# ScalarE issues the gate and up loads of the experts on its own queue, SyncE the down loads alone

## The chip, the cores and the metric

The kernel runs on 1 core of one Trainium2 chip. The metric is the device time of one execution in microseconds (us). Engines are named as the profile names them: PE (TensorE, the matmuls), PEld (its weight loads), DVE (VectorE), ACT (ScalarE), POOL (GpSimd) and SP (SyncE); a "q" behind a name is the engine's sequencer, which issues DMAs and waits on semaphores.

## What is computed

One step of a decoder layer over 264 tokens: 256 of a prompt and 8 samples. A token mixer with four branches comes first, then a mixture of 64 SwiGLU experts, of which every token takes 8, with one shared expert beside them. The part that matters here:

```python
def moe_ffn(h, router_w, router_bias, e_gate, e_up, e_down, s_gate, s_up, s_down):
    scores = jax.nn.sigmoid((h @ router_w).astype(jnp.float32))
    ...
    gates = jnp.zeros((n, N_EXPERTS), jnp.float32).at[jnp.arange(n)[:, None], idx].set(w)
    hg = jnp.einsum('nd,edf->nef', h, e_gate)
    hu = jnp.einsum('nd,edf->nef', h, e_up)
    act = jax.nn.silu(hg) * hu * gates[:, :, None].astype(h.dtype)
    routed = jnp.einsum('nef,efd->nd', act, e_down)
```

d is 1024 and f is 256, all in float32, so each expert has a gate, an up and a down matrix of 1,024 KB each, and the 64 experts together 201 MB. Every expert's weights are read from HBM once.

## The kernel before

The mixer and the routing take the first 350 us or so, and the change leaves them alone. After them the experts run as 64 jobs in 16 groups of four: job `4*i + j` is place `j` (0 to 3) of group `i`. The routing sorts the experts by how many tokens chose them, and the order of the jobs is written to `order_i`, one row of 64 integers; the first two jobs are experts 0 and 1. A job takes 128, 64 or 32 rows (CAP, HALF, QUARTER), a fixed size for each place. A middle group ("full group", i from 3 to 13) has rows of 128, 32, 64 and 32; the last group (i = 15) has four jobs of 32.

Weights go to `wexp`, which has four slots of 6,144 numbers per partition: gate in 0:2048, up in 2048:4096, down in 4096:6144. Job `4*i + j` uses slot `j`. Two semaphores a slot tell of landings: `gu_full[j]` (gate and up) and `down_full[j]`.

PE's order is written out by hand in `body` (line 1381 on): for each place `j` it computes `up(i, j)` (lines 1253, 1256, 1258 and 1259, by the size of the job) and in its middle turns the activation of the job before (`turn_act`, L898); then come the token list of the job four places on (L1206), the sums of a sheet at one place of each group (L1341), and the turning of gathered rows (`turn_rows`, L898 on `xn`); last is `down` of the job before (L1290, L1299, L1305 and L1308). So `down` of a job follows `up` of the next one. `up` counts `up_done` once, `down` counts `down_done` twice.

ACT goes beside it: `act_out` (L1660), `gate_out` (the silu, L1668), `rows_out` (L1652, half of the turned rows to `mid`) and `y_out` (L1682, L1685). DVE multiplies (L2248), copies the other half of the rows (L2229) and splits the outputs (L2263). POOL gathers the rows of tokens of a sheet from `h_table` to `xn` (L824), two sheets a group.

The loads come all from SP, on one queue. After the first four jobs' loads, `reload(i, s)` (line 679) runs for each job from 4 on: it loads the expert's number into a register, waits until `up` of the job four places before is done, and issues gate and up (L661, L662); then it waits until `down` of the job five before is done and issues the down load (L665) of the job before. The queue then holds gate, up, down of the job before, gate, up, and so on. After the last job come `turn_first_sums` (L1350, L1364), the last `down` and `last_sum` (L1316), final norm and the store.

Of the kernel before, what the change touches and what calls it, by code (L numbers as in the profile page):

```python
# [26 lines left out]
NE = 64  # L27
# [77 lines left out]
def bank_of(name):  # L105

    return (JOB[name] + FIRST_BANK) % NBANK, JOB[name] // NBANK
# [18 lines left out]
UNROLL = 4  # L126
# [31 lines left out]
def bass_decoder_step(nc, x_prompt, x_sample, state_conv, state_pool, state_conf, c_prompt, c_sample,  # L158
# [6 lines left out]
    with ExitStack() as ctx:  # L165
        def sb(name, shape, dt=F32):
            return ctx.enter_context(nc.sbuf_tensor(name, shape, dt))
# [3 lines left out]
        def sb_twin(name, shape):  # L171

            t = sb(name, shape)
            at = nc.sbuf_base - 4 * int(np.prod(shape[1:]))
            twins[name] = nc.alloc_sbuf_tensor_at(name + "_r", shape, F32R, offset=at)
            return t
# [5 lines left out]
        def sem(name):  # L182
            return ctx.enter_context(nc.semaphore(name))
# [5 lines left out]
        wexp = sb_twin("wexp", [P, UNROLL, SLOTF])  # L189
# [83 lines left out]
        order_i = sb("order_i", [1, NE], I32)  # L273
# [93 lines left out]
        S = {n: sem(n) for n in names}  # L367
        gathered = [sem(f"gathered{b}") for b in range(2)]
        gu_full = [sem(f"gu_full{s}") for s in range(UNROLL)]
# [6 lines left out]
        def await_full(eng, name):  # L376

            b, before = bank_of(name)
            eng.wait_ge(bank_full[b], before + 1)
            return psum[:, b, :]  # L380
# [5 lines left out]
        def await_freed(eng, name):  # L386

            b, before = bank_of(name)
            eng.wait_ge(bank_free[b], before + 1)
# [5 lines left out]
        def need(eng, sem_, value):  # L395

            if not isinstance(value, int) or value > 0:
                eng.wait_ge(sem_, value)
# [58 lines left out]
        def rows_used(i, j):  # L457

            if isinstance(i, int) and i == 0:
                return ROWS_OF_FIRST_JOB[j]  # L460
            if last_group(i):
                return QUARTER
            return (ROWS_OF_END_JOB if end_group(i) else ROWS_OF_LIGHT_JOB if light_group(i) else ROWS_OF_JOB)[j]
# [13 lines left out]
        def first_group(i):  # L477

            return isinstance(i, int) and i == 0

        def light_group(i):

            return isinstance(i, int) and 0 < i <= LIGHT_FIRST or end_group(i) or last_group(i)
# [26 lines left out]
        def sheet_of(i, s):  # L510

            return s if first_group(i) else 2 * i + 1 + s

        def buffer_of(i, s):

            return s % 2 if first_group(i) else 1 - s

        def next_sheet(i, j):

            if j == UNROLL - 1:  # L520
                return None if isinstance(i, int) and i == LAST else (i + 1, 0)
            if first_group(i):
                return (0, 2) if j == 1 else None
            return (i, 1) if j == (1 if light_group(i) else 0) else None

        def jobs_before_buffer(i, s):

            if first_group(i):
                return 1 if s == 2 else 0
            if s == 1:  # L530
                return UNROLL * i
            return UNROLL * (i - 1) + (2 if first_group(i - 1) or light_group(i - 1) else 1)
# [15 lines left out]
        def slots_of(i, j):  # L548

            return max(rows_used(i, j), HALF)  # L550

        gate_v = e_gate[0].rearrange("e (p k) f -> e p (k f)", k=KT)
        up_v = e_up[0].rearrange("e (p k) f -> e p (k f)", k=KT)
# [26 lines left out]
        def _(sp):  # L580
# [33 lines left out]
            for i, u in enumerate(SPLIT):  # L614
# [9 lines left out]
                n, at = divmod(i - FIRST_BRANCH, PER_BRANCH)  # L624
# [24 lines left out]
            def rows_of_expert(view, e):  # L649
                return view[e] if isinstance(e, int) else view[bass.ds(e, 1)].rearrange("e p n -> (e p) n")  # L650

            def expert_of(i, j):

                if isinstance(i, int) and i == 0 and j < FIXED:
                    return j
                at = UNROLL * i + j
                entry = order_i[0:1, at:at + 1] if isinstance(i, int) else order_i[0:1, bass.ds(at, 1)]
                return sp.value_load(entry, min_val=0, max_val=NE - 1)

            def load_gate_up(e, s):  # L660
                sp.dma_start(wexp[:, s, 0:2048], rows_of_expert(gate_v, e)).then_inc(gu_full[s], 16)  # L661
                sp.dma_start(wexp[:, s, 2048:4096], rows_of_expert(up_v, e)).then_inc(gu_full[s], 16)  # L662

            def load_down(e, s):
                sp.dma_start(wexp[:, s, 4096:6144], rows_of_expert(down_v, e)).then_inc(down_full[s], 16)  # L665
# [6 lines left out]
            for s in range(FIXED, UNROLL):  # L672
                e = expert_of(0, s)
# [2 lines left out]
                load_gate_up(e, s)  # L676
                load_down(e, s)

            def reload(i, s):
                n = UNROLL * i + s  # L680
                e = expert_of(i, s)
                sp.wait_ge(S["up_done"], n - 3)
                load_gate_up(e, s)
                pi, ps = (i if s else i - 1), (s - 1) % UNROLL
                if isinstance(pi, int) and pi == 0:
                    return
                before = expert_of(pi, ps)
                sp.wait_ge(S["down_done"], 2 * (n - 4))
                load_down(before, ps)

            for s in range(UNROLL):
                reload(1, s)
            with sp.Fori(2, NE // UNROLL) as i:
                for s in range(UNROLL):
                    reload(i, s)
            final = expert_of(NE // UNROLL - 1, UNROLL - 1)
            sp.wait_ge(S["down_done"], 2 * (NE - 4))
            load_down(final, UNROLL - 1)

            def extra(r, job, n):  # L700
                sp.wait_ge(S["x_xt"], n + 1)
# [13 lines left out]
            for m, t in enumerate(FINAL_ORDER):  # L715
                t0, n = TILES[t]
# [734 lines left out]
        def _(ac):  # L1451
# [171 lines left out]
            for m, t in enumerate(MIX_ORDER):  # L1623
                t0, n = TILES[t]
# [20 lines left out]
            def shared_silu(j):  # L1645
                b = await_full(ac, ("shared_gate", j))
                free(F(sh_silu[:, j, :], b[:, 0:TOK], ACT.Silu), ("shared_gate", j))

            def rows_out(i, s):
                ac.wait_ge(S["xt_done"], sheet_of(i, s) + 1)  # L1650
                need(ac, S["up_done"], jobs_before_buffer(i, s))
                F(xgT[buffer_of(i, s)][:, 0:4, :], psum[:, 5, :].rearrange("p (k c) -> p k c", k=4), ACT.Copy).then_inc(S["xgt_act"], 1)  # L1652

            def act_out(i, j):
                e = UNROLL * i + j
                n = rows_used(i, j)
                ac.wait_ge(S["tact_done"], e + 1)
                need(ac, S["down_done"], 2 * e - 2)
                at = HALF if n == QUARTER else 2 * P
                F(actT[:, j % 2, :, 0:n], psum[:, 2, 0:at].rearrange("p (h c) -> p h c", h=2)[:, :, 0:n], ACT.Copy).then_inc(S["actT_ready"], 1)  # L1660

            def gate_out(i, j):
                e = UNROLL * i + j
                n = slots_of(i, j)
                width = P if rows_used(i, j) == QUARTER else FE
                ac.wait_ge(S["up_done"], e + 1)
                need(ac, S["act_ready"], e - 1)
                F(silu[0:n, j % 2, 0:width], psum[CAP - n:CAP, j % 2, 0:width], ACT.Silu).then_inc(S["silu_ready"], 1)  # L1668
# [38 lines left out]
            def body(i, first=False, last=False):  # L1707
                for j in range(UNROLL):
                    prev = not (first and j == 0)
                    pi, pj = (i if j else i - 1), (j - 1) % UNROLL  # L1710
                    if prev:
                        act_out(pi, pj)
                    gate_out(i, j)
                    if next_sheet(i, j):
                        rows_out(*next_sheet(i, j))
                    if last and j:
                        raw_out(pj)
                    elif prev:
                        y_out(pi, pj)
# [2 lines left out]
            rows_out(0, 0)  # L1722
            shared_silu(1)
            await_full(ac, ("shared_up", 1))
            rows_out(0, 1)
            body(0, first=True)
            body(1)
            for i in range(2, LOOP_FROM):
                body(i)
# [17 lines left out]
            for m, t in enumerate(FINAL_ORDER):  # L1747
                n = TILES[t][1]
# [776 lines left out]
```

## Time and profile before

| | |
|---|---|
| median of 3 runs | 887.52 us (885.96 to 888.55) |
| the profiled execution | 888.6 us |
| its span, first to last instruction | 886.8 us |
| granted clock of TensorE, mean | 0.983 of full speed |
| PE busy | 838.4 us (95%) |
| DVE busy | 571.4 us (64%) |
| ACT busy | 309.3 us (35%) |
| DMA | 295.93 MB, mean 334 GB/s |
| the SP queue's part of it | 280.55 MB, 81.9% of 16 engines |

The time of the whole execution is compared with the median; the trace counts from the first instruction, so its times are read against the span. Busy PE means that matmuls are in its pipeline, not that it is at its peak. DMA-issuing instructions are not counted as busy time of an engine. "To landing" is the time from the issue of a DMA to the semaphore that tells that all of it has arrived. Line numbers are those of the kernel before; the change moves those behind it by a few.

### The profile page before, as it was taken

The page shows a single profiled execution, that of the slowest core. Times are in us where ns is not written, and L with a number is a line of the kernel's source. Part 1 is how long each engine was busy: PE and PEld are TensorE (multiplying, and loading weights), DVE is VectorE, ACT ScalarE, POOL GpSimd, SP SyncE. Part 2 cuts the span into 40 slices and gives each one's busy share as a digit, 9 for nine tenths or more (in the row PEclk, how much of TensorE's full clock was granted, in tenths as well). Part 3 has the DMA queues.
Part 4 walks back from the last instruction along what each step waited for, and adds up shares of the span by engine and source line. Part 5 has one row for each costly group of instructions (what it writes and reads, how often), then busy time and mean ns, then how long its engine had stood idle before and what let it go on. Part 6 is the DMA issues. An engine that isn't in the chain of part 4 may idle for free.

```text
span 886.8 us, 21212 instructions
## 1 busy us (share of the span) xinstructions
PE 838.4 (95%) x7938; PEld 638.9 (72%) x7938; DVE 571.4 (64%) x1431; ACT 309.3 (35%) x592; POOL 49.1 (6%) x92
## 2 busy tenths in 40 slices
PE   4799999999999999999999999999999999998794
PEld 2599999999999998757675656656665656566471
DVE  2458888899996787546664555546464655555555
ACT  3464444343428423022332323232232323222324
POOL 2010000000000000110000000000000000000000
PEclk9999999999999999899999999999999999999997
DMA  9995557788977645989999999999999999999961
GB/s 339 345 257 157 168 179 238 253 308 263 331 264 258 199 174 226 389 320 404 404 421 419 418 420 420 420 421 421 420 419 421 422 419 419 419 418 420 418 266 50
DMA packets 92711, 295.93 MB, mean 334 GB/s; under 512 B 7718, under 2 KB 45670, under 8 KB 67659
## 3 DMA queue, kind: packets, MB, share of 16 engines
q1 hardware_dynamic: 86139, 280.55, 81.9%
q0 software_dynamic: 6016, 13.10, 4.0%
q10 hardware_dynamic: 489, 1.33, 0.5%
q8 instruction: 48, 0.79, 0.4%
q14 instruction: 19, 0.16, 0.0%
HBM read 300.19 MB, written 4.14 MB: 343 GB/s over the span
## 4 chain that ended last, share of the span: by engine, by line
PE 69%; DVE 14%; DMA 12%; issue 2%; ACT 1%; SPq 1%; DVEq 0%; POOLq 0%; ACTq 0%
PE psum L894 19%; PE psum L1256 9%; DMA wexp<-in_e_up 9%; PE psum L1341 6%; PE psum L898 6%; PE psum L1253 6%; PE psum L1258 6%; PE psum L1299 4%; DVE mid L1922 4%; DVE wexp_r L1795 4%; PE psum L1290 3%; PE psum L1305 3%; DMA xn<-h_table,idx 2%; DMA wexp<-in_ada_w 2%; PE psum L1316 1%
## 5 line engine op out<-in xcount | busy, mean ns | idle before, releaser
L894 PE MATMUL psum<-xn_r,wexp_r 128*128 128x264 f32 x1024 | 193.8, 289 | 6.0 <-DVE hT_r L1833 6.0
L894 PEld LDWEIGHTS psum<-xn_r,wexp_r 128*128 128x128 f32 x1024 | 161.8, 191 | 8.4 <-issue 8.0
L894 PE MATMUL psum<-hT_r,wexp_r 128*128 128x264 f32 x512 | 146.4, 286 | 0.0
L1795 DVE TENSOR_TENSOR wexp_r<-wexp,wexp_r 128x1024 fp32r<-128x1024 f32 x88 | 106.6, 1217 | 22.1 <-ACT wexp_r L1505 21.7
L1505 ACT ACTIVATE wexp_r<-wexp 128x1024 fp32r<-128x1024 f32 x88 | 92.3, 1054 | 59.5 <-PE psum L894 44.3
L894 PEld LDWEIGHTS psum<-hT_r,wexp_r 128*128 128x128 f32 x512 | 98.0, 191 | 0.1
L1256 PE MATMUL psum<-wexp,mid 128*128 128x512 f32 x208 | 94.8, 600 | 0.6 <-DMA wexp<-in_e_up 0.6
L2187 DVE TENSOR_SCALAR idx<-psum 32x1 int32<-32x1 f32 (+2 forms) x62 | 13.4, 216 | 118.4 <-PE psum L1206 117.3
L1253 PE MATMUL psum<-wexp,mid 128*32 128x128 f32 x2112 | 76.3, 284 | 10.9 <-DMA wexp<-in_e_up 8.6
L2263 DVE TENSOR_TENSOR bc_r<-psum,xn_r 32x256 fp32r<-32x256 f32 (+2 forms) x136 | 65.9, 484 | 27.4 <-ACT xn_r L1685 17.5
L1253 PEld LDWEIGHTS psum<-wexp,mid 128*32 128x32 f32 x2112 | 58.8, 110 | 26.9 <-issue 15.1
L1256 PEld LDWEIGHTS psum<-wexp,mid 128*128 128x128 f32 x208 | 37.4, 190 | 48.5 <-issue 48.0
L894 PE MATMUL psum<-wexp_r 128*128 128x264 f32 (+1 forms) x512 | 71.5, 285 | 0.0
L1258 PE MATMUL psum<-wexp,mid 128*64 128x256 f32 x288 | 69.6, 385 | 0.3 <-DMA wexp<-in_e_up 0.3
L1259 PE MATMUL psum<-wexp,mid 128*64 128x256 f32 x288 | 69.6, 384 | 0.0
L894 PEld LDWEIGHTS psum<-wexp_r 128*128 128x128 f32 x512 | 66.8, 189 | 0.9 <-issue 0.9
L2305 DVE TENSOR_TENSOR mid<-mid,psum 128x264 f32<-128x264 f32 x120 | 50.7, 427 | 13.9 <-PE psum L1341 10.2
L1258 PEld LDWEIGHTS psum<-wexp,mid 128*64 128x64 f32 x288 | 36.9, 137 | 29.8 <-issue 12.9
L824 POOL DMA_INDIRECT xn<-h_table,idx x33 | 33.4, 1012 | 447.3 <-DVE idx L2187 209.2
L1341 PE MATMUL psum<-hT_r,mT_r 128*128 128x264 f32 x240 | 53.3, 304 | 0.6
L1668 ACT ACTIVATE hT<-psum 64x256 f32<-64x256 f32 (+2 forms) x64 | 20.8, 326 | 92.2 <-PE psum L1256 41.4
L1922 DVE SCALAR_TENSOR_TENSOR mid<-wexp,prm,mid 128x256 f32<-128x256 f32 x120 | 49.7, 474 | 0.0
(344 smaller groups left out, 1307.4 us busy)
## 6 DMA issues: line engine op xcount, KB each, us to landing
wexp<-in_e_gate SPq DMA_DIRECT2D x64, 1024.0 KB, 14.5
wexp<-in_e_up SPq DMA_DIRECT2D x64, 1024.0 KB, 17.5
wexp<-in_e_down SPq DMA_DIRECT2D x64, 1024.0 KB, 17.1
wexp<-in_w_in SPq DMA_DIRECT2D x32, 1024.0 KB, 6.3
mid<-in_ada_w SPq DMA_DIRECT2D x8, 2048.0 KB, 9.5
wexp<-in_w_branch SPq DMA_DIRECT2D x8, 1024.0 KB, 5.3
wexp<-in_ada_w SPq DMA_DIRECT2D x14, 512.0 KB, 10.7
wexp<-in_w_out SPq DMA_DIRECT2D x4, 1024.0 KB, 6.4
```

The costliest lines, as they stand in the source:

```text
L894: last = mm(out, a[x], b[y], start=start and x == y == 0, stop=stop and x == 1)
L898: return nc.tensor.transpose(out, src, ident[0:rows, 0:rows])
L1253: last = mm(psum[q * QUARTER:(q + 1) * QUARTER, j % 2, 0:P], x[:, k, :], w[:, k, 1 - q // 2, q % 2:FE:2], start=(k == 0), stop=(k == KT - ...
L1256: last = mm(psum[:, j % 2, :].rearrange("p (a f) -> p a f", a=2), x[:, k, :], w[:, k], start=(k == 0), stop=(k == KT - 1))
L1258: mm(psum[HALF:CAP, j % 2, 0:FE], x[:, k, :], w[:, k, 0], start=(k == 0), stop=(k == KT - 1), tile_position=(0, HALF))
L1259: last = mm(psum[0:HALF, j % 2, 0:FE], x[:, k, :], w[:, k, 1], start=(k == 0), stop=(k == KT - 1), tile_position=(0, 0))
L1341: last = mm(out, as_r(y[:, c * P:(c + 1) * P]), as_r(to_token[:, a, :]), start=((b, a) == sheets[0] and y is y_sheets[b][0] and not shared ...
L1505: F(as_r(high(u, q)), low(u, q), ACT.Copy).then_inc(S["w_hi"], 1)
L1795: V.tensor_tensor(as_r(low(u, q)), low(u, q), as_r(high(u, q)).bitcast(F32), ALU.subtract).then_inc(S["w_lo"], 1)
L1922: taps[c] = mark(V.scalar_tensor_tensor(dcv[:, c, 0:SEQ], gluP[:, c, h:h + SEQ], w, dcv[:, c, 0:SEQ], ALU.mult, ALU.add))
L2263: last = V.tensor_tensor(as_r(low[rows, a]), whole, as_r(high[rows, a]).bitcast(F32), ALU.subtract)
L2305: V.tensor_tensor(accT[:, c, :], accT[:, c, :], out, ALU.add).then_inc(S["sum_taken"], 1)
```

## The change

SP's `reload` is split. `reload_down` on SP waits until `down` of the job four places before is done (the last job that used the slot) and issues the down load of this job. A new `reload_gate_up` on ACT loads the expert's number and issues the two loads; it stands in ACT's `body` right behind `gate_out(i, j)` and is for job `j` of the next group. `gate_out` waits for `up` of the same slot's job, which was what SP waited for. ACT waits once for `order` to be written. The loads of jobs 0 to 3 stay on SP.

```diff
--- before.py
+++ after.py
@@ -676,26 +676,16 @@
                 load_gate_up(e, s)
                 load_down(e, s)
 
-            def reload(i, s):
-                n = UNROLL * i + s
+            def reload_down(i, s):
                 e = expert_of(i, s)
-                sp.wait_ge(S["up_done"], n - 3)
-                load_gate_up(e, s)
-                pi, ps = (i if s else i - 1), (s - 1) % UNROLL
-                if isinstance(pi, int) and pi == 0:
-                    return
-                before = expert_of(pi, ps)
-                sp.wait_ge(S["down_done"], 2 * (n - 4))
-                load_down(before, ps)
+                sp.wait_ge(S["down_done"], 2 * (UNROLL * (i - 1) + s + 1))
+                load_down(e, s)
 
             for s in range(UNROLL):
-                reload(1, s)
+                reload_down(1, s)
             with sp.Fori(2, NE // UNROLL) as i:
                 for s in range(UNROLL):
-                    reload(i, s)
-            final = expert_of(NE // UNROLL - 1, UNROLL - 1)
-            sp.wait_ge(S["down_done"], 2 * (NE - 4))
-            load_down(final, UNROLL - 1)
+                    reload_down(i, s)
 
             def extra(r, job, n):
                 sp.wait_ge(S["x_xt"], n + 1)
@@ -1659,6 +1649,14 @@
                 at = HALF if n == QUARTER else 2 * P
                 F(actT[:, j % 2, :, 0:n], psum[:, 2, 0:at].rearrange("p (h c) -> p h c", h=2)[:, :, 0:n], ACT.Copy).then_inc(S["actT_ready"], 1)
 
+            def reload_gate_up(i, j):
+
+                at = UNROLL * i + j
+                entry = order_i[0:1, at:at + 1] if isinstance(i, int) else order_i[0:1, bass.ds(at, 1)]
+                e = ac.value_load(entry, min_val=0, max_val=NE - 1)
+                for at, view in ((0, gate_v), (2048, up_v)):
+                    ac.dma_start(wexp[:, j, at:at + 2048], view[bass.ds(e, 1)].rearrange("e p n -> (e p) n")).then_inc(gu_full[j], 16)
+
             def gate_out(i, j):
                 e = UNROLL * i + j
                 n = slots_of(i, j)
@@ -1711,6 +1709,8 @@
                     if prev:
                         act_out(pi, pj)
                     gate_out(i, j)
+                    if not last:
+                        reload_gate_up(i + 1, j)
                     if next_sheet(i, j):
                         rows_out(*next_sheet(i, j))
                     if last and j:
@@ -1722,6 +1722,7 @@
             rows_out(0, 0)
             shared_silu(1)
             await_full(ac, ("shared_up", 1))
+            await_freed(ac, "order")
             rows_out(0, 1)
             body(0, first=True)
             body(1)
```

On ACT, in a light group (groups 1 and 2), from the silu of a job of 32 rows, or from the output copy behind it, to the row copy behind the silu of the next job, which has 64. TENSOR_LOAD reads the expert's number into a register, ISA rows are small register instructions. Before:

```order
L1668 ACTIVATE hT<-psum 64x128
L1685 ACTIVATE xn_r<-psum 64x512 x2
L1660 ACTIVATE hT<-psum 128x2x32
L1668 ACTIVATE hT<-psum 64x256
L1652 ACTIVATE mid<-psum 128x512
```

and now:

```order
L1683 ACTIVATE xn_r<-psum 64x512 x2
L1650 ACTIVATE hT<-psum 128x2x32
L1666 ACTIVATE hT<-psum 64x256
L1656 TENSOR_LOAD order_i
L1656 ISA x2
L1658 ISA
L1658 DMA wexp<-in_e_gate 128x2048
L1658 DMA wexp<-in_e_up 128x2048
L1642 ACTIVATE mid<-psum 128x512
```

Between each silu and what ACT does next stand now a load of the number and two DMA issues.

On SP, in its loop over the groups, one job. Before:

```order
L661 DMA wexp<-in_e_gate 128x2048
L662 DMA wexp<-in_e_up 128x2048
L658 ISA
L658 TENSOR_LOAD order_i
L658 ISA x2
L688 ISA
L665 ISA
L665 DMA wexp<-in_e_down 128x2048
```

and now:

```order
L658 ISA
L658 TENSOR_LOAD order_i
L658 ISA x2
L681 ISA
L665 ISA
L665 DMA wexp<-in_e_down 128x2048
```

SP issues one DMA a job where there were three, and no gate or up load stands ahead of a down load on its queue.

## Rows read from the trace of the kernel before

**Rows 1.** The page's 40 slices: DMA share in tenths, GB/s.

```profile
DMA  9995557788977645989999999999999999999961
GB/s 339 345 257 157 168 179 238 253 308 263 331 264 258 199 174 226 389 320 404 404 421 419 418 420 420 420 421 421 420 419 421 422 419 419 419 418 420 418 266 50
```

**Rows 2.** Windows: us, busy us (x instructions) by engine, PEclk, DMA share, GB/s.

```profile
370.00:390.00 20.00, 20.00 (x71) 9.71 (x70) 8.34 (x35) 2.94 (x6) 3.08 (x4) 1.00 0.84 328
550.00:600.00 50.00, 49.80 (x514) 30.28 (x511) 27.89 (x83) 16.48 (x41) 3.98 (x4) 1.00 1.01 421
800.00:840.00 40.00, 32.86 (x401) 21.50 (x399) 22.13 (x64) 12.63 (x31) 2.99 (x3) 0.96 1.02 418
850.00:860.00 10.00, 8.12 (x173) 5.66 (x173) 7.44 (x14) 4.48 (x13) 0.00 (x0) 1.00 0.65 271
```

**Rows 3.** The chain of waits, first full-size job two groups apart: start, us, work.

```profile
618.36 3.63 PE psum L1256 x8
679.50 3.63 PE psum L1256 x8
```

**Rows 4.** DMA queues, 640 to 700 us: packets, MB, share of 16 engines.

```profile
q1 hardware_dynamic: 3278, 23.87, 95.6%
q0 software_dynamic: 576, 1.36, 5.9%
```

**Rows 5.** Landings (400:450, 750:800, all of the page); PE's wait for a pair.

```profile
wexp<-in_e_gate SPq DMA_DIRECT2D x7, 1024.0 KB, 8.8
wexp<-in_e_gate SPq DMA_DIRECT2D x7, 1024.0 KB, 21.3
wexp<-in_e_down SPq DMA_DIRECT2D x64, 1024.0 KB, 17.1
PE psum L1253 <- DMA wexp<-in_e_up: 8.6, 3, 4.1
```

**Rows 6.** Job 63's issues on SP; landing of its up, then its down.

```profile
829.84 0.34 SPq L661 DMA_DIRECT2D wexp<-in_e_gate  x1
830.28 1.26 SPq L662 DMA_DIRECT2D wexp<-in_e_up  x1
DMA to landing us min/median/max: 26.1/26.1/26.1
837.90 0.34 SPq L665 DMA_DIRECT2D wexp<-in_e_down  x1
DMA to landing us min/median/max: 23.4/23.4/23.4
```

**Rows 7.** Timeline of PE in the last group: start us, us, work.

```profile
841.79 1.43 PE L1253 MATMUL psum<-wexp,mid 128*32 128x128 f32 x32 [4.12 <-DMA wexp<-in_e_up]
854.10 1.07 PE L1290 MATMUL psum<-wexp,hT 128*32 128x256 f32 x16
856.65 0.89 PE L1253 MATMUL psum<-wexp,mid 128*32 128x128 f32 x23 [1.49 <-DVE hT L2248]
864.19 1.07 PE L1290 MATMUL psum<-wexp,hT 128*32 128x256 f32 x16
```

**Rows 8.** SP's load of a number, 600:640; ACT's silu and row copy.

```profile
L658 SPq TENSOR_LOAD <-order_i x10: 263/268/274, 600.8 to 639.1; - x10
625.65 0.38 ACT L1668 ACTIVATE hT<-psum 128x256 f32<-128x256 f32 x1 [3.20 <-PE psum L1256]
626.63 0.60 ACT L1652 ACTIVATE mid<-psum 128x512 f32<-128x512 f32 x1 [0.59 <-PE psum L898]
```

**Rows 9.** Gather L824 in traffic, its rows turned; last its landing without traffic.

```profile
616.84 1.00 POOL L824 DMA_INDIRECT xn<-h_table,idx  x1 [19.78 <-DVE idx L2187]
DMA to landing us min/median/max: 8.2/8.2/8.2
625.45 1.14 PE L898 MATMUL psum<-ident,xn 128*128 128x128 f32 x8
DMA to landing us min/median/max: 3.4/3.4/3.4
```

## The prediction

> **What bounds the kernel now.** I read the page's 40 slices first. From slice 18, about 395 us, to slice 38 the DMA row stands at 9 and the rate at some 420 GB/s [rows 1]; the windows show PE as full there, 49.80 of 50 us between 550 and 600 [rows 2]. So two things are full at once in the expert part, and the share of busy time does not tell which sets the end. The windows at its edges do: the DMA share is 0.84 in 370 to 390 us, 1.01 from 550 to 600, 1.02 from 800 to 840, and 0.65 in 850 to 860, where the loads run out; PE, full in the middle, is busy only 32.86 of the 40 us from 800 [rows 2]. PE is the faster of the two by a little. Its period of a group of four experts is (679.50 - 618.36) / 2 = 30.6 us [rows 3]. The loads of a group are 12 transfers of 1,024 KB, 12.6 MB; the SyncE queue moves 23.87 MB in 60 us [rows 4], 0.398 MB/us, so a group takes 31.6 us. Hence the queue of loads grows longer: from issue to landing a gate load takes 8.8 us between 400 and 450 us and 21.3 us between 750 and 800 [rows 5]. Late in the run the load becomes what PE waits for: PE waits three times for a gate and up pair in its quarter-row jobs, 8.6 us together [rows 5]. The last ones decide the end. **The stream of loads, never idle after about 390 us, sets when job 63 can begin, and from there a tail follows that does not depend on loads.**
>
> Now the end in detail. The up weights of job 63 are issued at 830.28 and land 26.1 us later, at 856.4; its down weights are issued at 837.90 and land 23.4 us later, at 861.3, the end of the stream [rows 6]. Between these two landings lie exactly two transfers, the downs of 62 and 63: 1.05 MB at 420 GB/s is 2.5 us each, and 2 x 2.5 = 5.0 against 4.9 seen. That is the order of one first-in, first-out queue: gate, up, then the down of the job before. PE begins job 61 at 841.79 when its pair lands, adds sums and turns rows, and begins job 63 at 856.65, after an idle 1.49 us that ends with the landing at 856.4 (the view names VectorE, which had been done) [rows 7]. From 856.65 to the end of the span at 886.8 are 30.1 us of tail.
>
> **The change, part by part.** It removes no byte and no wait of PE. It moves 120 gate and up transfers (60 jobs) to ScalarE's queue; SyncE keeps 64 downs and the first four pairs.
>
> 1. *Issue is later.* SyncE had the expert's number in a register before the wait ended. ScalarE first issues its silu (0.38 us for a full job), then loads the number, 0.27 us, with small instructions that I put at 0.45 us (an estimate), then issues [rows 8]. Against the end of the up product that is 0.38 + 0.27 + 0.45 = 1.1 us later. With 8 to 21 us of loads in front of it the delay is hidden 58 or 59 times. It is not hidden at job 4's pair, near 379 us, where the DMA share is 0.84 [rows 2]: **+1.1 us** on the whole stream. The bounds are 0.4 (silu does not block the sequencer) and 2.
>
> 2. *ScalarE is later with what follows.* The copy L1652 starts 0.6 us after the silu ends (625.65 + 0.38 to 626.63) [rows 8]; with 0.7 us of loading and two issues of 0.34 us or a little more [rows 6] it starts some 0.8 us later, after 1.4 us in place of 0.6. PE's next quarter-row job waits for it, so PE's period may go from 30.6 to about 31.2, still under 31.6. Nothing on the stream: +0. If the period went over 31.6, the queue of loads would still have to run dry first.
>
> 3. *The order of the stream changes.* The DMA engines no longer have one order. How they share is seen with the gather, which is on a third queue: issued at 616.84, with more than 15 us of loads ahead of it, it lands after 8.2 us [rows 9]. It does not queue behind them; the engines take turns. I therefore take it that both load queues get equal shares while both have work. A down needs a third of the bytes and is offered half, so downs come through in some 5 to 7 us instead of over 20, and the gate and up pairs pay for it. In the middle this costs nothing: no slot stands empty, the bytes are the same and there is always work. At the end it does. All downs, the last among them (issued 837.90 or a little later), are in before the last pair, so the pair of job 63 is the last to land, at the end of the stream: 861.3 + 1.1 = 862.4 instead of 856.4. By this alone job 63 starts 862.4 - 856.65 = 5.7 us later. Second bound: the pairs of 61 to 63 are back to back. If no down was left between them, pair 61 lands two pairs, 10.0 us, before 862.4, at 852.4. From the start of 61 PE needs its own 13.4 us to the point where 63 may start (841.79 to the end of L1290 at 855.17, with 63 following) [rows 7], so 63 would start at 865.8, 9.1 us later. Downs that are issued late because PE is late still lie between the pairs, so pair 61 lands earlier than that: I take the middle, **+7.5 us** with the 1.1 us in it, with 5.7 and 9.1 as bounds.
>
> 4. *The gather has another rival.* The gather at 616.84 lands at 625.0 and PE turns its rows at 625.45 [rows 9]: a slack of 0.4 us in each full group. Without load traffic one takes 3.4 us [rows 9], so one busy queue costs it 4.8. A second busy queue costs between 0 (the down queue is empty then) and another 4.8. Half of a down's time overlaps it, so I take 1 to 2 us. That makes PE's period about 32.5, 0.9 over the stream's 31.6: over 11 full groups it eats 10 us of a backlog that begins at 8 to 10 us. So it is just hidden, with **+0.5 us** for what leaks.
>
> The sum is 7.5 + 0.5 = +8 us. The profiled execution took 888.6 us (span 886.8), 1.1 above the median of 887.52; so 896.6 there, **895.5 us** as a median. A measurement here tells about 0.3%, 2.7 us, from no change.
>
> **The rivals.** *B, the gather binds.* If two busy queues double what one costs, the gather takes 13 us, PE's period is 30.6 + 4.4 + 0.6 = 35.6 at worst and 33.5 with half of it. At 33.5 the 11 full groups lose 11 x 1.9 = 21 us, less the backlog of 8 to 10: +11 to +13 beyond the order's cost, about 906; at worst over 925. For it: the slack of 0.4 us. Against it: a down then stands in its queue only a third to a half of the time.
>
> *C, no difference.* The transfers may be taken in the order of their issue whatever the queue, since both kinds are made by the same hardware. Then only the 1.1 us stays: 888.6. The Trainium skill, "DMA: Bandwidth & Descriptors", section "Issuing engines are not separate DMA queues", says that DMAs started by several engines run on the same 16 engines and interleave, and that this saves only the issuing sequencer's time. By that rule the result would be no change, since SyncE's issue time is on no path; the gather's early landing [rows 9] bears out the interleaving, which is just what lets a down overtake, so I give it little.
>
> *D, faster.* If the queue with the pairs gets more than two thirds of the bytes while both are busy (it holds two transfers for each down), the pairs overtake the downs. Pair 63 was behind the downs of 60 and 61, which could still wait: it would land 5.0 us sooner, at 851.4, and the downs of 62 and 63, of which PE takes the first at 864.19 [rows 7], would land at 861.3 as now and just fit. Job 63 starts 5 us sooner: 882.5. The point is the two-thirds share. Against it: nothing in the trace shows a preference.
>
> **How the numbers follow.** A, the overtaking order as worked out (891 to 900): 0.56. B: 0.18. C: 0.14. D: 0.12. The range leaves out D and the far end of B, together 0.2: 885.5 to 906. Slower by over 0.3% is A and B, 0.74; within it C, 0.14; faster D, 0.12.
>
> **What would show it.** Right: the median landing of e_down falls from 17.1 us [rows 5] to 5 to 8, that of e_gate grows; the last down lands before the last pair; PE waits for pairs from some earlier point on, with more than the 8.6 us; DMA share still 1.0 up to about 860; the span from job 63's start to the end still 30 us. B shows as PE waiting for xn<-h_table in L898 and a DMA share under 1 in 500 to 800. C shows the old landings, D a pair that lands in under 15 us late in the run. The prediction is wrong if downs do not land early or if the stream moves at another rate than 420 GB/s with two queues: 1% of 470 us is 4.7 us, either way.

## The result and the profile after

The changed kernel takes **922.53 us** in the median of four runs (918.33 to 925.34), the kernel before 886.74 in the runs beside it: ratio 1.0405, 95% interval 1.0369 to 1.0441. It is 36 us slower. The direction was forecast; the size was not: 895.5 us, with 906 as the upper end.

The profiled execution took 925.34 us, its span 923.6, which is 36.8 over the span before. First the slices of the page, to be laid beside [rows 1]: DMA share, rate, and the clock that PE was granted.

```profile
DMA  9984567898777629899999999999999899998961
GB/s 341 334 249 141 184 185 250 267 321 267 266 251 259 223 97 383 328 405 395 420 419 380 369 409 364 375 405 367 390 421 357 357 410 368 377 408 346 419 262 49
PEclk9899999999999998999999999999999899999998
```

The DMA row is no longer full. From slice 21 (counted from 0) the rate lies at 346 to 410 GB/s in most slices where some 420 stood before. The clock row is too coarse to tell much (a 9 is all from 90% up); the mean granted clock of the execution is 0.964, before 0.983. The windows say more, beside [rows 2]; the last one is 860 to 880 us, since the loads now end about 894.

```profile
370.00:390.00 20.00, 20.00 (x72) 10.16 (x71) 8.24 (x33) 2.34 (x5) 3.08 (x4) 1.00 0.87 326
550.00:600.00 50.00, 47.11 (x443) 29.95 (x439) 25.41 (x73) 11.91 (x30) 1.99 (x2) 0.97 0.94 376
800.00:840.00 40.00, 37.05 (x318) 22.12 (x318) 18.57 (x53) 10.41 (x25) 1.99 (x2) 0.96 0.93 367
860.00:880.00 20.00, 18.38 (x272) 12.02 (x271) 12.38 (x34) 8.21 (x20) 1.00 (x1) 1.00 1.02 417
```

The stream starts as before (0.87 against 0.84 between 370 and 390 us), falls to 0.94 in the middle, where PE is also less busy (47.11 of 50 us, before 49.80), and is full again near the end, 1.02. So in the middle neither the loads nor PE are at their limit: something else sets the pace. Of the DMA queues and issues, q1 is SyncE's and q10 is ScalarE's:

```profile
q1 hardware_dynamic: 68859, 154.72, 46.3%
q10 hardware_dynamic: 17769, 127.17, 34.0%
wexp<-in_e_down SPq DMA_DIRECT2D x64, 1024.0 KB, 9.7
wexp<-in_e_gate ACTq DMA_DIRECT2D x60, 1024.0 KB, 8.1
wexp<-in_e_up ACTq DMA_DIRECT2D x60, 1024.0 KB, 12.0
```

The change does what it says: 126 MB moved from SyncE's queue to ScalarE's (127.17 MB there, 1.33 before). Downs land after 9.7 us in place of 17.1 [rows 5], gates after 8.1. Short landings look like an improvement and are the opposite here: fewer loads are waiting in line, because PE asks for them later. Who PE waits for:

```profile
PE psum L888 <- DMA xn<-h_table,idx: 28.4, 11, 3.1
PE psum L1243 <- DMA wexp<-in_e_up: 3.7, 2, 2.1
```

**The wait for the gather is new**, 28.4 us in 11 times, one for each of the 11 full groups (before it was 0.6 us in all in this view). The waits are 2.1 to 3.1 us long. One of them in detail, after [rows 9]: the pair's issue on ScalarE, the gather of the second sheet, the down load behind it, the landing of the gather, and then PE.

```profile
568.59 0.48 ACTq L1658 DMA_DIRECT2D wexp<-in_e_up  x1
569.19 1.00 POOL L814 DMA_INDIRECT xn<-h_table,idx  x1 [24.22 <-PE psum L888]
570.68 0.34 SPq L665 DMA_DIRECT2D wexp<-in_e_down  x1
DMA to landing us min/median/max: 11.2/11.2/11.2
580.47 1.89 PE L888 MATMUL psum<-ident,xn 128*128 128x128 f32 x8 [2.77 <-DMA xn<-h_table,idx]
582.29 1.94 PE L1280 MATMUL psum<-wexp,hT 128*32 128x256 f32 x16
```

The gather is issued at 569.19 and lands 11.2 us later, not 8.2; in the 11 full groups this gather takes 10.5 to 11.3 us. PE turns its rows right then, at 580.47, after 2.77 us of idling. The second loss is in the durations: turning eight blocks takes 1.89 us, before 1.14 [rows 9], and the down product of a quarter job 1.94, before 1.07 [rows 7]. Windows of one microsecond show why (the third number from the end is the granted clock):

```profile
579.00:580.00 1.00, 0.00 (x0) 0.00 (x0) 0.07 (x1) 0.00 (x0) 0.75 (x1) 1.00 1.01 418
580.00:581.00 1.00, 0.53 (x3) 0.53 (x4) 0.00 (x0) 0.00 (x0) 0.00 (x0) 0.84 1.03 434
581.00:582.00 1.00, 1.00 (x7) 0.96 (x5) 0.00 (x0) 0.00 (x0) 0.00 (x0) 0.50 1.00 418
583.00:584.00 1.00, 1.00 (x12) 0.39 (x8) 0.58 (x4) 0.00 (x0) 0.00 (x0) 0.50 0.97 401
585.00:586.00 1.00, 1.00 (x27) 0.80 (x23) 0.90 (x3) 0.94 (x4) 0.00 (x0) 1.00 1.06 422
649.80:655.00 5.20, 5.20 (x97) 4.00 (x98) 3.29 (x10) 2.76 (x7) 0.00 (x0) 1.00 1.01 417
```

Before the wait and in it the clock was 1.00. PE idles from 577.7 to 580.47, and from 580.5 to 584 the granted clock is 0.50, the 1.2 GHz level in place of 2.4. What PE does there takes nearly twice as long, a loss of 0.16 + 3 x 0.50 + 0.05 = 1.7 us. Such a stretch of 3.4 us follows ten of the eleven waits, and one of the ten is twice as long; behind the wait that ends at 649.71 there is none, as the last line shows. So the number of half-speed stretches is part of an execution's time: the four executions of the changed kernel took 918.33 us at a mean clock of 0.972, and 922.32 to 925.34 us at 0.964 to 0.968.

The period of a group, read from the gather of group 4 to that of group 12, is (776.86 - 499.56) / 8 = **34.7 us**, before 30.6 [rows 3]:

```profile
499.56 1.22 POOL L814 DMA_INDIRECT xn<-h_table,idx  x1 [24.80 <-PE psum L888]
776.86 1.00 POOL L814 DMA_INDIRECT xn<-h_table,idx  x1 [23.83 <-PE psum L888]
```

The loads need 31.6 us a group [rows 4], so PE is now the slower one, and the stream of loads has holes. The account of the 36.8 us, by the start of PE's first product of a full-size job: at group 4 PE is 5.0 us late (500.62 against 495.59), at group 13 it is 41.7 late (813.31 against 771.63), so 36.7 us are lost over nine groups; then 4.3 us are given back, since the kernel before had to wait for loads in this stretch and this one less, and the tail from job 63's start is 0.5 us shorter. 5.0 + 36.7 - 4.3 - 0.5 = 36.9.

At the end, the issue of the last down load, its time to landing, and job 63 on PE, beside [rows 6] and [rows 7]:

```profile
877.55 0.34 SPq L665 DMA_DIRECT2D wexp<-in_e_down  x1
DMA to landing us min/median/max: 12.2/12.2/12.2
893.98 1.36 PE L1243 MATMUL psum<-wexp,mid 128*32 128x128 f32 x32 [2.13 <-DMA wexp<-in_e_up]
```

The last down lands at 877.55 + 12.2 = 889.75; PE has waited for the pair of job 63 until 893.98. Before, the pair landed first, 4.9 us ahead of the last down. That part of the forecast came true; what it costs by itself is measured below.

### The profile page after: what moved, and what is told of

It is laid out like the page before. It is cut to its first block and busy times, and to the rows that moved or that the text cites. A ratio compares the mean times of both kernels' runs of the same rounds, so it can differ in the third digit from the quotient of the medians.

```text
span 923.6 us, 21191 instructions
## 1 busy us (share of the span) xinstructions
PE 852.3 (92%) x7938; PEld 647.9 (70%) x7938; DVE 571.5 (62%) x1431; ACT 309.2 (33%) x593; POOL 49.7 (5%) x92
## 3 DMA queue, kind: packets, MB, share of 16 engines
q10 hardware_dynamic: 17769, 127.17, 34.0%
## 5 line engine op out<-in xcount | busy, mean ns | idle before, releaser
L1243 PE MATMUL psum<-wexp,mid 128*32 128x128 f32 x2112 | 78.6, 291 | 4.7 <-DMA wexp<-in_e_up 3.7
L888 PE MATMUL psum<-ident,xn 128*128 128x128 f32 (+1 forms) x312 | 50.7, 313 | 28.5 <-DMA xn<-h_table,idx 28.4
L1243 PEld LDWEIGHTS psum<-wexp,mid 128*32 128x32 f32 x2112 | 62.2, 115 | 21.1 <-issue 12.0
L888 PEld LDWEIGHTS psum<-ident,xn 128*128 128x128 f32 (+1 forms) x312 | 42.5, 197 | 32.1 <-issue 24.4
L2306 DVE TENSOR_TENSOR mid<-mid,psum 128x264 f32<-128x264 f32 x120 | 50.5, 427 | 13.2 <-PE psum L1331 9.2
L1642 ACT ACTIVATE mid<-psum 128x512 f32<-128x512 f32 x33 | 19.7, 597 | 116.0 <-PE psum L888 115.6
```

The lines of the kernel that those rows point to most:

```text
L888: return nc.tensor.transpose(out, src, ident[0:rows, 0:rows])
L1243: last = mm(psum[q * QUARTER:(q + 1) * QUARTER, j % 2, 0:P], x[:, k, :], w[:, k, 1 - q // 2, q % 2:FE:2], start=(k == 0), stop=(k == KT - ...
L2306: V.tensor_tensor(accT[:, c, :], accT[:, c, :], out, ALU.add).then_inc(S["sum_taken"], 1)
```

## The experiments

The theory after the traces (G): with two load queues busy, the gather gets a smaller share of the DMA engines and lands 3 us late; PE waits, and its clock falls behind most of the waits. The rivals: ScalarE's own time for its new work (R), and the later issue of the pairs (O). All runs were set against the kernel before, run beside them on the same chip: 887.01 us for the first four, 886.4 for the next four, 886.93 for the last two.

### One queue again, on ScalarE

SyncE's `reload_down` and its two loops are taken out of the changed kernel, and ScalarE gets one of its own, called behind `y_out`:

```diff
-            def reload_down(i, s):
-                e = expert_of(i, s)
-                sp.wait_ge(S["down_done"], 2 * (UNROLL * (i - 1) + s + 1))
-                load_down(e, s)
...
+            def reload_down(i, j):
...
+                ac.dma_start(wexp[:, j, 4096:6144], down_v[bass.ds(e, 1)].rearrange("e p n -> (e p) n")).then_inc(down_full[j], 16)
...
                     elif prev:
                         y_out(pi, pj)
+                        reload_down(pi + 1, pj)
```

> The kernel after the change, but ScalarE issues the down loads too (behind the output copy of the same job) and SyncE issues none: one queue again, in the order of the kernel before, and ScalarE carries even more issue work than after. Theory G (a second busy load queue makes the gather land late, PE waits for it and its clock falls): the gather comes back from 11.0 to about 8.2 us, PE's wait for it from 28.4 us to near 0, the time to 886 to 893 us. Rival R (ScalarE's own time for loading numbers and issuing delays its copies and so PE): the time stays at 920 us or grows, the gather wait being only where the delay shows. Rival O (the pairs are issued 1 to 2 us later, behind the silu, and this starves the stream): stays near 920 us as well.

888.86 us (886.18 to 893.84, 10 runs), ratio to before 1.0024 (1.0002 to 1.0045). The share of ScalarE's queue, the gathers' median landing between 500 and 760 us, and PE's wait for them:

```profile
q10 hardware_dynamic: 26409, 190.09, 51.9%
xn<-h_table,idx POOLq DMA_INDIRECT x17, 8.3
PE psum L877 <- DMA xn<-h_table,idx: 0.7, 2, 0.5
```

ScalarE issues everything here, more than in the changed kernel, and behind the silu as there. R and O fall: the loss is not in where the loads are issued but in their standing on two queues. The 2 us over the kernel before is near the 1.1 us that the prediction put on the later issue.

### ScalarE's time alone

The kernel before, all loads on SyncE as there, with a register load and three small copies added on ScalarE at the place where the change issues its pair:

```diff
                     gate_out(i, j)
+                    if not last:
+                        same_time(i + 1, j)
...
+            def same_time(i, j):
+                ac.value_load(entry, min_val=0, max_val=NE - 1)
+                for pad in (cmean, lower, ones):
+                    f = F(pad[:, :], zeros[:, :], ACT.Copy)
```

> The kernel before, all loads on SyncE, but ScalarE behind each silu loads the expert's number and makes three small copies of a dead tile (128x128, about 0.2 us each), some 1.2 to 1.5 us in all, as long as its number load and two issues in the kernel after. Rival R: a large part of the 36 us, over 900 us. Theory G: the time stays at 886 to 890 us, PE's period at 30.6 to 31.5 us, under what the loads take.

886.76 us (884.82 to 888.76, 10 runs), ratio 1.0003 (0.9988 to 1.0018). In the trace the three copies end some 1.1 us behind the silu (in the changed kernel the row copy starts 1.5 us behind it), so the imitation is a little short; the run before this one has the whole of the new work, and more. A microsecond of work for ScalarE in each job costs nothing that can be measured. It lies beside the stream of loads, as the second term of the prediction had it.

### The down queue kept empty during the gather

```diff
                 sp.wait_ge(S["down_done"], 2 * (UNROLL * (i - 1) + s + 1))
+                if s in (1, 2):
+                    sp.wait_ge(gathered[0], 16 * (i + 2))
                 load_down(e, s)
```

> The kernel after the change, but SyncE holds the down loads of places 1 and 2 of each group until the gather of that group's second sheet has landed, so that the down queue is empty while this gather is under way; two queues otherwise as after. Theory G: this gather lands in about 8.2 to 8.7 us, PE's wait for it nearly vanishes, the period of a group comes back from 34.6 to 31 to 32 us and the time to 890 to 900 us (the last pair still lands after the last down, as in the kernel after). Rival R (ScalarE's own time) and rival O (the late issue of the pairs): no gain, 918 us or more, since only down loads are made later.

896.85 us (896.64 to 897.73), ratio 1.0122 (1.0098 to 1.0145). So 26 of the 36 us come back when two downs a group wait for the gather. PE's wait for it is nearly gone, and the start of job 63 now stands bare:

```profile
PE psum L890 <- DMA xn<-h_table,idx: 1.1, 3, 0.5
864.66 1.94 PE L1245 MATMUL psum<-wexp,mid 128*32 128x128 f32 x32 [5.45 <-DMA wexp<-in_e_up]
```

Job 63 begins at 864.66, with its pair landing there, after 5.45 us of waiting. This is the case that the prediction's third term described (862.4 to 865.8, before 856.65), and the time is within 1.4 us of the 895.5 forecast. What the forecast left out is what this experiment took away.

### One down held in place of two

```diff
-                if s in (1, 2):
+                if s == 2:
```

> As the run that held the downs of two places, but only place 2's is held, the one issued 1.5 us behind the gather; place 1's, issued some 4 us ahead of it, is still on its way beside it. If the bytes of the down queue beside the gather set its landing, this one lands between the two, 9 to 10.5 us, and the time lies between 897 and 922, at about 905 us. If it is 897, only the down behind the gather mattered; if 920, only the one ahead of it.

894.61 us (893.08 to 896.73), ratio 1.0089 (1.0072 to 1.0105). I expected the gather's landing and the time between those of the two runs. They are not: the gather of the second sheet, its landing, and the down, which SyncE issues once it has landed:

```profile
589.39 1.00 POOL L816 DMA_INDIRECT xn<-h_table,idx  x1 [20.40 <-PE psum L890]
DMA to landing us min/median/max: 8.3/8.3/8.3
597.82 0.34 SPq L665 DMA_DIRECT2D wexp<-in_e_down  x1
```

8.3 us. Only the down that is issued 1.5 us *behind* the gather mattered, not the one issued 4 us ahead of it. The traces show why. The first packet of the gather moves 4.2 us after its issue in the kernel before, in the changed kernel and here alike; what differs is how long its packets then take: they are through 7.6 us after the issue before, 10.5 us in the changed kernel, 7.8 us here. In the changed kernel all three queues are busy in that time (MB moved between 574 and 580 us):

```profile
q10 hardware_dynamic: 160, 1.16, 46.0%
q1 hardware_dynamic: 156, 1.08, 42.9%
q0 software_dynamic: 127, 0.32, 13.2%
```

The two load queues get nearly the same, 1.16 and 1.08 MB, and 0.32 MB of the gather pass between them. The down issued ahead (565.17, landed 575.4) shares only the first 2 us; the one issued at 570.68 stands there all the rest. With this one held, the down queue is empty in the four microseconds (593.5 to 597.5 us) in which all 144 packets of the gather move:

```profile
q10 hardware_dynamic: 182, 1.34, 80.8%
q0 software_dynamic: 144, 0.33, 21.6%
q1 hardware_dynamic: 16, 0.00, 0.2%
```

The held down now moves beside the gather of the other sheet, which lands after 10.5 us and more; but PE wants those rows only some 9 us after that, and nothing is lost.

### The clock's part: PE kept busy while it waits

```diff
+                if s == 1 and not first_group(i) and not light_group(i):
+                    for _n in range(8):
+                        mm(psum[:, 5, :], ident[:, :], x_sb[:, 0, 0:512], start=True, stop=True)
                 pe.wait_ge(gathered[at], 16 * (1 + s // 2 if first_group(i) else i + 1 + s))
```

> The kernel after the change, but PE makes eight more products (128x128 by 128x512, about 3.5 us together, results overwritten) where it would wait for the gather of the second sheet in the full groups. The wait stays, the work is added. If the fall of the granted clock to half behind each wait costs the 1.7 us a group that the trace shows (turn and down product 1.9 us each instead of 1.1), the time falls to 900 to 910 us, with granted clock 0.98 instead of 0.964. If the clock costs nothing on the path, it stays at 922 us or grows by what the products take over the wait, 0.7 us a group, to 930.

951.95 us (950.18 to 954.28), ratio 1.0741 (1.0709 to 1.0774). A miss of mine: an fp32 product of 512 columns is two passes, so eight are 16 passes of 0.43 us, 7.1 us on PE, of which only 2.8 fit into the wait. 4.3 us too many less 1.7 for the clock is 2.6 us a group, and 11 x 2.6 = 29, against 29.4 measured. The repeat with three products:

```diff
-                    for _n in range(8):
+                    for _n in range(3):
```

> As the run that kept PE busy, with three added products in place of eight (one product turned out to be two passes, 0.43 us each, so three last about 2.6 us, a little less than the 2.8 us that PE waits for the gather of the second sheet). If the clock is the second part of the loss, PE's clock stays at full speed behind the wait, 1.7 us are saved in each full group and the time falls by 11 x 1.7 = 19 us to 900 to 908 us. If it is not, the time stays at 918 to 926 us.

909.38 us (906.87 to 910.41), ratio 1.0252 (1.0231 to 1.0274). The three added products, then the turning and the down product behind them:

```profile
573.39 2.82 PE L1208 MATMUL psum<-x_sb,ident 128*128 128x512 f32 x6
576.25 1.16 PE L888 MATMUL psum<-ident,xn 128*128 128x128 f32 x8
577.34 1.07 PE L1283 MATMUL psum<-wexp,hT 128*32 128x256 f32 x16
```

The wait is filled with useless work, the gather lands as late as in the changed kernel (11.0 us), yet the kernel is 13.2 us faster than the changed one, because the turning takes 1.16 us again and the down product 1.07: the granted clock stays at 1.00 from 400 us to 870. The time lies just over the range that I gave, whose 19 us supposed that nothing of the 1.7 us a group is lost again. So of the 36 us some 13 are the clock (1.2 us in each of 11 groups; the added work outlasts the wait a little in places, which takes some of the 1.7), and some 23 are the wait itself and the order at the end.

### The queues exchanged

SyncE issues the pairs, as in the kernel before, and ScalarE the downs:

```diff
-            def reload_down(i, s):
+            def reload(i, s):
+                n = UNROLL * i + s
                 e = expert_of(i, s)
-                sp.wait_ge(S["down_done"], 2 * (UNROLL * (i - 1) + s + 1))
-                load_down(e, s)
+                sp.wait_ge(S["up_done"], n - 3)
+                load_gate_up(e, s)
...
-                    if not last:
-                        reload_gate_up(i + 1, j)
...
                     elif prev:
                         y_out(pi, pj)
+                        reload_down(pi + 1, pj)
```

> The two queues exchanged: SyncE issues the pairs as in the kernel before, at once when the up product ends, and ScalarE issues the down loads behind the output copy of the same job. Two load queues share the engines, ScalarE has one issue a job. Theory G: the gather lands in 10 to 11 us and the time is 910 to 922 us. Rival: if it mattered that the pairs stood behind the silu on ScalarE, 886 to 895 us.

909.46 us (908.18 to 915.05), ratio 1.0279 (1.0241 to 1.0317). PE's wait for the gather, and the window from 500 to 800 us:

```profile
PE psum L889 <- DMA xn<-h_table,idx: 23.7, 11, 2.8
500.00:800.00 300.00, 280.57 (x2613) 173.80 (x2612) 153.92 (x444) 81.01 (x198) 17.94 (x18) 0.98 0.98 400
```

Pairs on SyncE, at once, downs on ScalarE: the wait is there again, 23.7 us in 11 times, and the rate is 400 GB/s. It is somewhat cheaper than the change as made: the waits are 4.7 us shorter in all, and only five of the eleven are followed by a half-speed stretch (ten in the changed kernel). Two queues are the cause here too. The median lies just under the range that I gave.

### The order of the last loads

```diff
                 sp.wait_ge(S["down_done"], 2 * (UNROLL * (i - 1) + s + 1))
+                if isinstance(i, int) and i == LAST:
+                    sp.wait_ge(gu_full[min(s + 1, UNROLL - 1)], 32 * (LAST + 1))
                 load_down(e, s)
...
-            with sp.Fori(2, NE // UNROLL) as i:
+            with sp.Fori(2, LAST) as i:
...
+            for s in range(UNROLL):
+                reload_down(LAST, s)
```

The last group is taken out of SyncE's loop, so that the wait can stand in it alone. With both downs held for the gather as well:

> As the run that held the downs of two places, and in the last group each down load is also held until the pair of the next job has landed, which gives the end of the stream the order of the kernel before. Theory: what is left of the loss there (896.85 against 887.01) is the order of the last loads, so the last pair lands 2.5 to 5 us before the end of the stream instead of with it, and the time falls to 891 to 894 us. If the rest was not the order but a slower or later stream, no gain.

891.55 us (888.71 to 893.0), ratio 1.0065 (1.0048 to 1.0082): 5.3 us less than with the holds alone (4.7 when each is set against the kernel before in its own runs), what the order was expected to be worth and a little more. By itself, with nothing held for the gathers:

> The kernel after the change; only the last group's down loads are held until the pair of the next job has landed, nothing is held for the gathers. In the kernel after the last pair landed at 893.7 us, after the last down at 889.8, and PE waited 2.1 us for it, having come late itself. If the two costs do not add where PE is already late, this brings back no more than about 2 us: 919 to 923 us. If the order of the last loads were a large part of the 36 us, 914 us or less.

912.86 us (911.41 to 915.0), ratio 1.0301 (1.0275 to 1.0327), 9.7 us under the changed kernel where I expected 2 at most. From the first product of group 13 to job 63 it takes 4.3 us less than the changed kernel (76.4 against 80.7), which is the order: near the end the jobs are small, PE needs less than the loads again (the DMA share of 1.02 from 860 to 880 us shows it), and so the two losses add. The rest comes earlier, where this kernel loads and computes as the changed one does; its groups take 34.0 us there, not 34.7. In the traces this is the clock and the waits: PE waits 25.6 us for gathers in place of 28.4, and only six of the eleven waits are followed by a half-speed stretch, in place of ten. Here is one without:

```profile
713.00:719.00 6.00, 5.71 (x100) 4.51 (x101) 3.68 (x12) 2.75 (x7) 0.55 (x1) 1.00 1.01 418
```

Two single executions of equal mean clock agree with it: at 0.972 this kernel took 915.0 us and the changed one 918.33, 3.3 us apart, near the 4.3 of the order. Why the clock falls behind fewer of the waits here is **open**.

### The smallest mend of both

In `reload_down`, with the last group again out of the loop:

```diff
...
+                if s == 2:
+                    sp.wait_ge(gathered[0], 16 * (i + 2))
+                if isinstance(i, int) and i == LAST:
+                    sp.wait_ge(gu_full[min(s + 1, UNROLL - 1)], 32 * (LAST + 1))
```

> Both mends at their smallest: only place 2's down is held until the second sheet's gather has landed, and in the last group each down until the pair of the next job has landed. From 894.61 us with the first alone the time should fall by 3 to 5 us, to 889.5 to 892 us; it should not beat the kernel before (886 to 887), since the loads still are as many and the pairs are issued a microsecond later. If it beats the kernel before, the two queues are worth something that the traces do not show.

888.1 us (887.04 to 890.46, 10 runs), ratio 1.002 (1.0007 to 1.0033), a little under the range that I gave. The window from 500 to 750 us is full again, clock and DMA:

```profile
500.00:750.00 250.00, 244.22 (x2322) 150.53 (x2321) 135.60 (x392) 71.85 (x176) 15.95 (x16) 1.00 1.01 420
```

With two waits the two queues are as good as one, to 0.2%, and not better. No run beat the kernel before. In the expert part its limit is the bytes at 420 GB/s, and none of these kernels changes their number or the rate.

## Why the prediction was wrong

**What bounds the kernel**: right. The stream of loads sets the end as long as PE's period stays under 31.6 us. I wrote that PE is the faster "by a little"; how little, 1.0 us a group, was the number that everything hung on.

**Term 1, later issue, +1.1 us**: right as far as can be measured. With everything else undone the kernel is 1.0024 times before (1.0002 to 1.0045).

**Term 2, ScalarE's time, +0**: right, 1.0003 (0.9988 to 1.0018).

**Term 3, the order at the end, +7.5 us with term 1**: right. The two load queues share equally, the last pair lands last, and the run that leaves only this gives +9.8 us (1.0122) with two downs held and +8.2 (1.0089) with one. Giving the old order back to the last group is worth some 5 us with both held and 6.5 with one. One detail was off: downs come through in 9.7 us, not in 5 to 7, since one often stands behind another on its own queue (565.17 landed at 575.4, the next was issued at 570.68). And in the changed kernel itself, where PE was late, the gate loads did not get slower as forecast, but faster, 8.1 us for 14.5.

**Term 4, the gather, +0.5 us**: this step failed. Its mechanism was named; its size was wrong in three places, one of them a cost put at nothing.
1. The gather lost 2.9 us, not "1 to 2". I counted the time a down stands in its queue as a half. The trace of before would have told that from group 4 on the down of place 2 is issued 1.7 us behind the gather every time, and that the gather's first packet moves 4.2 us after its issue, so that this down always stands there when the gather's bytes move. An average over phases was used where the phase is fixed.
2. PE's own wait was taken as all of the cost. Behind ten of the eleven waits the clock fell to half for 3.4 us, which cost 1.7 us more each time; 13.2 us came back when the waits were filled with products. Nothing in my sum had it, though the wait was in it. The trace of before shows this price too, behind the wait of 4.12 us that ends at 841.79 [rows 7]:

```profile
843.00:845.00 2.00, 2.00 (x34) 1.50 (x33) 0.00 (x0) 0.22 (x1) 0.00 (x0) 0.50 1.01 422
```

3. The cover was overrated. "0.9 us over the stream's 31.6, eaten from a backlog of 8 to 10 us" is sound for a period of 32.5. At 34.7 the excess is 3.1 us a group, 34 us over 11 groups, and the backlog is gone after three.

Rival B was the right mechanism, and its own arithmetic the right kind (a period of 33.5 to 35.6, 906 to over 925). It got 0.18, and the range was cut through the middle of it. With a slack of 0.4 us beside a transfer whose time under one busy queue had risen by 4.8, I would now have given it nearer a half, a judgement and not a measurement. C and D fell: the old landings did not stay, and neither queue is preferred. With C falls, for this kernel, what the Trainium skill says in "DMA: Bandwidth & Descriptors", section "Issuing engines are not separate DMA queues", as far as one reads from it that a second queue changes nothing but the issue time: that the transfers interleave, the trace bears out; here the interleaving cost 36 us, by the gather and by the order of the last loads.

## What to carry to other kernels

Moving transfers to a second queue added no bandwidth here (420 GB/s with one queue and with two), it changed who overtakes whom: list every small transfer that has little slack (here one gather with 0.4 us), and look at which transfers are always in flight beside it, by their phase in the loop and not by their mean share. When a wait of a few microseconds is new on TensorE, look in the granted clock for half-speed stretches behind waits that the trace already has, and add their price. And where two limits lie within 3% of each other, a cost that "has cover" is covered for that 3% only.

## What the runs showed of the hardware

- A gather of 0.3 to 0.4 MB landed 3.3 us after its issue with next to no load traffic (changed kernel, 378.89 us), about 8.2 us with one busy load queue, 10.5 to 11.3 us with two. With loads under way its first packet moved 4.2 us after its issue, whether one load queue was busy or two, and only the time of its packets grew. So a load issued 1.5 us behind it could still delay it, and one issued 4 us ahead did not.
- Two busy load queues moved nearly the same in 6 us, 1.16 and 1.08 MB.
- Idle stretches of 2.1 to 3.1 us on PE were followed by 3.4 us at a granted clock of 0.50 in ten of eleven cases in the changed kernel, in six of eleven and five of eleven in two kernels near to it. Useless products in those stretches kept the clock up and made the kernel 13.2 us faster (922.53 to 909.38) at an unchanged landing time.
